# One barrier-free section for the front of the third block, and 64-by-64 inverses of four heads at once

## The reference

```python
h = _layer_norm(x, ln_in_g, ln_in_b)
proj = h @ w_in
pool_in, qkv, z, beta_raw, a_raw, gate_a, gate_b = split(proj)
y_a = _multiscale_pool(pool_in, pool_w, pool_scale)     # windows 2, 4, 8, 16; 4 groups
...
# _gated_deltanet, 8 heads of 128, chunks of 64 tokens
qkv = silu(causal_depthwise_conv(qkv, conv_w))          # 4 taps, 24 tiles of 128 features
q = l2norm(q) * 128 ** -0.5 ; k = l2norm(k)
beta = sigmoid(beta_raw)
g = -exp(a_log) * softplus(a_raw + dt_bias)
a = strict_lower((k*beta) @ k.T * decay) + eye(64)      # one per head and chunk
sol = triangular_solve(a, [v*beta, k*beta*exp(gc)])
# then a scan over the 8 chunks of 64 tokens
...
mixed = sigmoid(gate_a) * y_a + sigmoid(gate_b) * y_b
h = _layer_norm(ALPHA * h + mixed @ w_out, ln1_g, ln1_b)
mlp = square(relu(h @ w_up)) @ w_down                   # and a gated sum, a last layer norm
```

## Time and profile before

| | |
|---|---|
| median of 3 executions | 3611.22 us (3601.39 to 3617.31) |
| the profiled execution | 3615.51 us, of which the span of its instructions is 3613.7 us |
| PE busy | 3304.1 us, 91% of the span |
| PE weight loads busy | 2606.9 us, 72% |
| DVE busy | 1746.7 us, 48% |
| ACT busy | 1216.6 us, 34% |
| POOL busy | 145.5 us, 4% |
| mean granted TensorE clock | 0.937 of full speed |

### The profile page before, as it was taken

How to read it: one execution, slowest core, us unless ns; L and a number is a source line. 1 busy time by engine, 2 the same in 40 slices (tenths; PEclk the granted TensorE clock), 3 DMA queues, 4 the chain that set the end, 5 groups by cost and what they waited for, 6 DMA issues and landing times. The chain is left out here.

```text
span 3613.7 us, 43046 instructions
## 1 busy us (share of the span) xinstructions
PE 3304.1 (91%) x17800; PEld 2606.9 (72%) x17800; DVE 1746.7 (48%) x2642; ACT 1216.6 (34%) x1751; POOL 145.5 (4%) x176
## 2 busy tenths in 40 slices
PE   8999997888699998998999999986977789999998
PEld 6888776667478886876557788865855668778885
DVE  4447536543354456767865333243643334553434
ACT  3333342222533333333443323232345222342323
POOL 0000000120000000000000000000002431000000
PEclk9999997869899999999999999998987988899999
DMA  3336321000223363322012233322220000223332
GB/s 135 97 96 216 111 79 35 2 2 8 82 71 99 117 204 128 97 79 64 1 49 86 82 95 98 99 64 64 88 88 18 19 25 20 75 82 99 94 99 94
DMA packets 76371, 285.23 MB, mean 79 GB/s; under 512 B 8464, under 2 KB 8592, under 8 KB 75152
## 3 DMA queue, kind: packets, MB, share of 16 engines
q1 hardware_dynamic: 76176, 282.47, 24.1%
HBM read 276.15 MB, written 6.29 MB: 78 GB/s over the span
## 5 line engine op out<-in xcount | busy, mean ns | idle before, releaser
L149 DVE TENSOR_TENSOR wlo<-raw,whi 128x1024 fp32r<-128x1024 f32 x450 | 552.2, 1227 | 1238.3 <-ACT whi L144 1238.0
L144 ACT ACTIVATE whi<-raw 128x1024 fp32r<-128x1024 f32 x450 | 475.9, 1058 | 1174.8 <-PE ps L173 1110.6
L171 PE MATMUL ps<-h_hi,wlo 128*128 128x512 f32 x1536 | 621.0, 404 | 51.2 <-PEq L80 21.2
L172 PE MATMUL ps<-h_lo,whi 128*128 128x512 f32 x1536 | 603.5, 393 | 0.0
L173 PE MATMUL ps<-h_hi,whi 128*128 128x512 f32 x1536 | 603.2, 393 | 0.0
L171 PEld LDWEIGHTS ps<-h_hi,wlo 128*128 128x128 f32 x1536 | 291.7, 190 | 130.6 <-issue 54.1
L172 PEld LDWEIGHTS ps<-h_lo,whi 128*128 128x128 f32 x1536 | 292.1, 190 | 62.0 <-issue 5.2
L173 PEld LDWEIGHTS ps<-h_hi,whi 128*128 128x128 f32 x1536 | 291.6, 190 | 62.0
L171 PE MATMUL ps<-mid_hi,wlo 128*128 128x512 f32 x784 | 307.4, 392 | 0.0
L173 PE MATMUL ps<-mid_hi,whi 128*128 128x512 f32 x784 | 305.0, 389 | 0.0
L172 PE MATMUL ps<-mid_lo,whi 128*128 128x512 f32 x784 | 305.0, 389 | 0.0
(11 more groups left out here) (580 smaller groups left out, 5135.9 us busy)
## 6 DMA issues: line engine op xcount, KB each, us to landing
raw<-in_wstream SPq DMA_DIRECT2D x453, 512.0 KB, 3.5
mod_ring<-in_wmod SPq DMA_DIRECT2D x48, 512.0 KB, 4.5
c_rows<-in_c_rows SPq DMA_DIRECT2D x3, 1024.0 KB, 5.6
x<-in_x_t SPq DMA_DIRECT2D x4, 512.0 KB, 7.7
x_saved<-x SPq DMA_DIRECT2D x1, 2048.0 KB, 8.9
x<-x_saved SPq DMA_DIRECT2D x1, 2048.0 KB, 9.1
mix_saved_d<-x SPq DMA_DIRECT2D x1, 2048.0 KB, 8.4
out<-x SPq DMA_DIRECT2D x8, 256.0 KB, 2.1
```

The lines of the kernel that those rows point to most:

```text
L144: act.activation(k.whi[:, n % SPLIT, :], k.raw[:, n % RAW, :], ACT.Copy).then_inc(k.hi_ready, 1)
L149: dve.tensor_tensor(k.wlo[:, n % SPLIT, :], k.raw[:, n % RAW, :], k.whi[:, n % SPLIT, :].bitcast(F32), ALU.subtract).then_inc(k.split_read ...
L171: pe.matmul(out, wlo, hi, start=first, stop=False)
L172: pe.matmul(out, whi, lo, start=False, stop=False)
```

## The change

The parts 1 to 3 above become one section, `branches_front`, with no barrier in it. The stream of weights is reordered for it: `ba`, eight tiles of q, the pool chunk, sixteen tiles of k and v, and then the eight chunks of `gate_a`. The running sums and the squares for the norms move to POOL; norms and pool go beside the q, k and v chunks, transposes and rows beside the `gate_a` chunks. `Background` has no slices there any more; `delta_matrices` takes 4 in each gap instead of 2. `invert` is called twice, for four heads, with 2 slices in each of its ten gaps; the scan keeps its 40.

```diff
-def invert(k, at, xt, tmp, bg=Idle(), slices=(0, 0)):
+def invert(k, at, xt, tmp, bg=Idle(), slices=(0, 0), pairs=4):
...
-        blocks = [(slice(64 * b, 64 * b + 64), slice(64 * p, 64 * p + 64)) for p in range(4) for b in range(2)]
+        tx, out = [k.ps[:, g, 0:width] for g in range(2)], [k.ps[:, 2 + g, 0:width] for g in range(2)]
...
+def branches_front(k, h, qkv, pool_in, mix, k_tok, v_tok, beta, nbeta, g, egc, ekg, egl, mix_d, mix_saved):
...
+        @m.block.gpsimd
+        def _(gp):
...
+            for i, w in enumerate(POOLS):
+                src, width = pool_in[:, i, :], 1
+                if i:
+                    gp.wait_ge(diff, 2 * i)
+                while width < w:
+                    dst = s[:, width.bit_length() % 2, :]
+                    if n:
+                        gp.wait_ge(step, n)
+                    gp.tensor_tensor(dst[:, pad:], src[:, pad:], src[:, pad - width:pad + SEQ - width], ALU.add)\
+                      .then_inc(step, 1)
+                    n += 1
+                    src, width = dst, 2 * width
+            for n in range(2 * DT):
+                gp.wait_ge(silu_done, n + 1)
+                if n >= 2:
+                    gp.wait_ge(sum_ready, n - 1)
+                gp.tensor_tensor(sq[:, n % 2, :], qkv[:, n, :], qkv[:, n, :], ALU.mult).then_inc(sq_ready, 1)
...
+        @m.block.tensor
+        def _(pe):
...
+            def square_sum(n):
+                pe.wait_ge(sq_ready, n + 1)
...
+                if n >= 4:
+                    pe.wait_ge(log_ready, n - 3)
+                    pe.wait_ge(pool_left, DT)
+                pe.matmul(k.ps[:, 4 + n % 4, :], mat(k, "ones"), sq[:, n % 2, :], start=True, stop=True)\
+                  .then_inc(sum_ready, 1)
...
+            def turn(n):
+                src, dst, i, T = tokens[n]
+                pe.wait_ge(normed, 2 * DT)
+                pe.wait_ge(silu_done, 3 * DT)
+                if n >= 2:
+                    pe.wait_ge(copied, n - 1)
+                for c in range(4):
+                    mm = pe.transpose(k.ps[:, 4 + n % 2, c * P:(c + 1) * P], src[:, 4 * i + c, T * P:(T + 1) * P],
+                                      mat(k, "ident"))
+                mm.then_inc(turned, 1)
+            pe.wait_ge(k.split_ready, b0 + 1)
+            chunk(b0, 4)
+            for f in range(3 * DT):
+                if f == DT:
+                    pe.wait_ge(k.split_ready, pool_chunk + 1)
+                    pe.wait_ge(d_lo, 4)
+                    pe.wait_ge(log_ready, 4)
+                    for o in range(DT):
+                        if o >= 4:
+                            pe.wait_ge(pool_left, o - 3)
+                        mm = products(k, pe, pool_chunk, k.ps[:, 4 + o % 4, :], dh[:, o // 2, :], dl[:, o // 2, :],
+                                      o * P, True, True)
+                        mm.then_inc(pool_done if o < DT - 1 else k.chunk_done, 1)
+                pe.wait_ge(k.split_ready, q_chunk(f) + 1)
+                if f >= 4:
+                    pe.wait_ge(pre_ready, f - 3)
+                chunk(q_chunk(f), f % 4)
+                group = (f - 5) // 4
+                if f >= 5 and f % 4 in (1, 2) and group < 4:
+                    first = 4 * group + 2 * (f % 4 - 1)
+                    square_sum(first)
+                    square_sum(first + 1)
+            for i in range(DT):
+                pe.wait_ge(k.split_ready, g0 + i + 1)
...
+                chunk(g0 + i, i % 4)
+                turn(2 * i)
+                turn(2 * i + 1)
+                if i == 3:
...
+                    for T in range(TT):
...
+                if i == 5:
...
+                            pe.matmul(k.ps[:, 7, 32 * b + 8 * T:32 * b + 8 * T + 8], mat(k, name), g[:, T, :],
+                                      start=True, stop=True)
...
+        @m.block.scalar
...
+            next_hi(k, act, b0)
+            act.activation(ba[:, :], k.ps[:, 4, :], ACT.Copy).then_inc(ba_kept, 1)
+            for f in range(3 * DT):
+                if f == DT:
+                    for o in range(DT):
+                        if o < DT - 1:
+                            act.wait_ge(pool_done, o + 1)
+                        else:
+                            next_hi(k, act, pool_chunk)
+                        act.activation(mix[:, o, :], k.ps[:, 4 + o % 4, :], ACT.Copy, scale=col(k, "pool_scale", o))\
+                           .then_inc(pool_left, 1)
+                next_hi(k, act, q_chunk(f))
+                if f == 0:
+                    act.wait_ge(zeroed, 1)
+                act.activation(pre[:, f % 4, 3:], k.ps[:, f % 4, :], ACT.Copy).then_inc(pre_ready, 1)
+                if f in (4, 5):
+                    for i in range(2 * (f - 4), 2 * (f - 3)):
...
+                act.wait_ge(tap_done, 4 * f + 4)
+                act.activation(qkv[:, f, :], qkv[:, f, :], ACT.Silu).then_inc(silu_done, 1)
+                if f >= 6 and f % 4 == 2 and f < 22:
+                    first = f - 6
+                    for n in range(first, first + 4):
+                        act.wait_ge(sum_ready, n + 1)
...
+                        act.activation(rs[:, n % 4, :], k.ps[:, 4 + n % 4, :], ACT.Ln, bias=k.eps[1e-6])\
+                           .then_inc(log_ready, 1)
+                    for n in range(first, first + 4):
+                        act.wait_ge(log_ready, n + 1)
+                        act.activation(rs[:, n % 4, :], rs[:, n % 4, :], ACT.Exp, scale=-0.5).then_inc(rs_ready, 1)
+            act.wait_ge(normed, 2 * DT)
+            for i in range(DT):
+                next_hi(k, act, g0 + i)
+                if i >= 4:
+                    act.wait_ge(mixed, i - 3)
+                act.activation(sig[:, i % 4, :], k.ps[:, i % 4, :], ACT.Sigmoid).then_inc(sig_ready, 1)
+                if i == 0:
+                    act.activation(ba[0:8, :], ba[0:8, :], ACT.Sigmoid).then_inc(beta_ready, 1)
+                if i == 1:
+                    act.activation(na[r, 0:1], col(k, "a_log")[r, :], ACT.Exp).then_inc(a_ready, 1)
...
+                    act.activation(ln[r, :], rc[r, :], ACT.Ln).then_inc(ln_ready, 1)
+                for n in (2 * i, 2 * i + 1):
...
+                    act.wait_ge(turned, n + 1)
+                    act.activation(dst[:, T, 512 * part:512 * part + 512], k.ps[:, 4 + n % 2, :], ACT.Copy)\
+                       .then_inc(copied, 1)
+            act.wait_ge(summed, 1)
...
+        @m.block.vector
         def _(dve):
...
+            def window(i):
+                w, u = POOLS[i], pool_in[:, i, :]
+                src = s[:, (w // 2).bit_length() % 2, :]
+                dve.wait_ge(step, steps[i])
+                dve.scalar_tensor_tensor(d[:, i, 16:], src[:, pad + 16:], 1.0 / w, u[:, pad + 16:], ALU.mult,
+                                         ALU.subtract).then_inc(diff, 1)
...
+            next_lo(k, dve, b0)
+            for f in range(3 * DT):
+                if f == DT:
+                    next_lo(k, dve, pool_chunk)
+                next_lo(k, dve, q_chunk(f))
+                dve.wait_ge(pre_ready, f + 1)
+                o = qkv[:, f, :]
...
+                        dve.tensor_scalar(o, x, w, None, ALU.mult).then_inc(tap_done, 1)
...
+                        dve.scalar_tensor_tensor(o, x, w, o, ALU.mult, ALU.add).then_inc(tap_done, 1)
+                if f < 4:
+                    window(f)
+                if f in (5, 6):
+                    for i in range(2 * (f - 5), 2 * (f - 4)):
+                        dve.wait_ge(d_hi, i + 1)
...
+                if f >= 8 and f % 4 in (0, 1):
+                    first = f - 8 + f % 4
+                    for n in range(first, first + 2):
+                        dve.wait_ge(rs_ready, n + 1)
+                        dve.scalar_tensor_tensor(qkv[:, n, :], qkv[:, n, :], P ** -0.5 if n < DT else 1.0,
+                                                 rs[:, n % 4, :], ALU.mult, ALU.mult).then_inc(normed, 1)
...
+            for i in range(DT):
+                next_lo(k, dve, g0 + i)
+                dve.wait_ge(sig_ready, i + 1)
+                dve.wait_ge(pool_left, i + 1)
+                dve.tensor_tensor(mix[:, i, :], mix[:, i, :], sig[:, i % 4, :], ALU.mult).then_inc(mixed, 1)
+                if i == 1:
...
+            dve.wait_ge(kept, 4)
+            dve.wait_ge(copied, 8)
...
-        with nc.sbuf_tensor(k.name("ba"), [P, 1, SEQ], F32) as ba:
-            dense(k, 1, DT, h, copy_out(k, ba), nothing)
-            bg = Background(k, ctx, 16, h, (6, 7), act_evac, dve_evac)
-            with stage(nc, "sent") as (block, sent):
-                @block.sync
-                def _(sp):
-                    sp.dma_start(mix_d, gate[:, :, :]).then_inc(mix_saved, 16)
-            gate_rows(k, ba, beta, nbeta, g, egc, ekg, egl, bg, 8)
-        norm_tiles(k, [qkv[:, t, :] for t in range(16)], lambda n: (P ** -0.5 if n < 8 else 1.0), 1.0, 1e-6,
-                   bg=bg, slices=4)
```

(56 more changed lines are left out.)

279 lines of the change are left out of this document (124 added, 155 removed).

## The result

The changed kernel takes **3548.7 us** (median of 4 executions, 3542.4 to 3551.5), against 3613.4 for the kernel before beside it. The ratio is 0.9825, interval 0.9808 to 0.9841. Forecast were 3560 and a range of 3530 to 3592. The profiled execution took 3550.1, its span 3548.2, its mean clock 0.942 against 0.937.

What follows compares the result with a forecast made beforehand. PE was taken to idle or run slow in the 531.8 us before the scan, q, k, v paced by an ACT-DVE ring; front 54 us less, matrices and inverses 2 more, so 52 less: 3560, range 3530 to 3592.

Steps and rivals of the forecast that it cites:

- pool chunk: Front, before tile 8's split: PE waits for ACT to empty a bank, then products and a q chunk; 11 us.
- front after Silu 23: Front's end: seven chunks, turns, transposes, row sums, PE restart and a wait, 55.5 us; then the tail, 10.6 us.
- The ring: Front's q, k, v chunks: ACT and DVE taking turns, not PE, set 5.64 us a round; 24 rounds, 135.4 us.
- The port: Front: POOL's 26 sums and squares hold up DVE by 0.4 us each, 10 us in all.
- The head start: Front before the ring starts: `ba` and first q chunk, 2 x 5.44 plus 2.4 for PE's restart, 13.3 us.
- The chunk ends: `delta_matrices`: six chunk ends, four ahead of an exponential at 2.9 us, two in last gaps at 3; 17.6 us.
- The inverses: Inverses: ten levels of 9.4 us for 20 of 4.91, other 10.1 us of each `invert` paid twice; 24 us less.
- the port's full price: Rival, front: each of POOL's 26 instructions costs DVE its full time, 27 us instead of 10; 3577; chance 0.15.
- the dear loads: Rival: each of eight exposed table switches costs its 1.28 us again, 10 us more; 3570; chance 0.02.
- a ring of sums and squares: Rival, front: each norms group waits a round for POOL, PE and ACT in turn; gain about 15 us, 3596; chance 0.05.
- PE at half clock: Rival, front: short idling keeps PE at half clock, 185 us more if in all 34 chunks, 3745; chance 0.03.
- the one where everything hides: Rival: no port cost in the front and chunk ends in the matrices free; 3532; chance 0.15.

Runs made afterwards that it cites:

- e2: Changed kernel with ACT's order turned: it splits tile f before the Silu of tile f-1, norms' groups moved by one tile; 3528.9 us, ratio 0.9777 to the kernel before.
- f3: Changed kernel with one table set holding both Ln and Exp loaded ahead of each group's four Ln; 3545.8 us, ratio 0.9816 to the kernel before.
- f2: Changed kernel with the pool chunk moved in two halves to before tiles 20 and 21, weight stream reordered to match; 3535.7 us, ratio 0.9789.
- e1: Changed kernel with the 16 squares of q and k moved from POOL to ACT's wait for the taps; 3548.9 us, ratio 0.9834 to the kernel before.
- f1: Changed kernel with ACT and DVE emptying a chunk's bank in the matrices after the step's exponentials and products, not before; 3538.4 us, ratio 0.9790.
- f8: f5 with f7's shift of slices added, so no chunk ends in a stage's last gap; 3489.5 us, ratio 0.9650 to the kernel before.
- u1: Changed kernel with the wide inverse undone: four narrow `invert` calls, front and matrices still changed; 3555.5 us, ratio 0.9851 to the kernel before.
- f6: e1 with the ten running sums left out too, so POOL does nothing beside the taps (pool branch computes something else); 3542.5 us, ratio 0.9805.
- f7: Changed kernel with one slice less in the last gap of the second and fourth `delta_matrices`, one more in the scan's second gaps; 3536.7 us, ratio 0.9782.
- f4: Changed kernel with the orders of e2, f1, f2 and f3 together; 3509.1 us, ratio 0.9713 to the kernel before.
- f5: f4 with the pool chunk's halves one tile later, at tiles 21 and 22; 3499.1 us, ratio 0.9683 to the kernel before.

## Why the prediction was right

3560 was 11 us high. Against the profiled execution the sum was 3563.5, measured 3550.1. By stretches all the differences went one way, 3.1 in the front, 2.1 in the matrices, 6.3 in the inverses and 2.0 in the stretches that the change doesn't touch, so the number is not owed to errors that cancel. By its terms:

| term | forecast | measured |
|---|---|---|
| `ba` and first q chunk | 13.3 | 11.0 |
| groups of Ln and Exp, four | 28.6 | 28.9 |
| pool chunk | 11 | 11.1 |
| PE late at tile 10 | 1.3 | 1.4 |
| POOL against DVE | 10 | 10.6 |
| front after Silu 23 | 66.1 | 64.2 |
| the whole front | 265.7 | 262.6 |
| four `delta_matrices` | 96.1 | 94.0 |
| inverses, change | -24 | -30.3 |
| all, change | -52 | -65.5 |

- **The ring.** 5.63 to 5.64 a round where nothing disturbs it (tiles 15 to 18 and 19 to 23). That it is a ring and not PE is shown by e2.
- **What is paid on it.** Norms and pool chunk came to a tenth. f3 shows a load as a part of it, at about its row; f2 shows that half of the pool chunk's 11 were waits for banks, and that the other half moves with the chunk. The measured sum of a row is the excess over 5.64 of the distances that it touches.
- **The port.** 10.6 for 26 instructions, 0.41 each, as I took it. That the sum came out is partly luck, as my even spread was wrong: 8.4 of it fall on the first six rounds. With the squares gone (e1) the ten running sums, one behind the other where DVE has windows to make, cost 5.2 (6.63, 7.28 and 8.22 over 5.63); the squares that queue behind them in the changed kernel most of the rest, and those of the last three groups 2.3. e1 gave 1.7 of its gain back at tiles 6 and 8 (6.68, 17.76). The Trainium skill (SBUF — State Buffer, "SBUF: two separate sides") has the port as an exclusive lock; the trace is in line with that, with the taps of a round at 5.8 in place of 2.8 us beside POOL's rows, and 5.63 or 5.64 in the first five rounds once POOL is idle.
- **Table loads.** f3 rules out the rival by which a switch costs more than its row. The Trainium skill (ScalarE: Activation LUTs, "What ACT_TABLE_LOAD costs") adds a drain of about 1380 ns; a load less gave 1.44 us, its row of 1.28 and little else.
- **The head start** was 2.3 shorter: the `ba` chunk was done 5.6 us after the start, without the 2.4 of a restart that the earlier trace rows had shown. PE had stood 3.2 us ahead of it, and 10.7 in the earlier trace rows. In the changed kernel PE came back at half clock (a matmul every 0.43 us instead of 0.23) after stands of 9.2 and 5.0 us at the pool chunk. No run varied the stand by itself.
- **The chunk ends** were taken at 17.6 for six. The four ahead of an exponential were put at 2.9 each, 11.6; f1 gained 10.9 by taking them out of the way, so the sum was right, but its spread of 0.6, 6.1, 3.5 and 0.6 was not what I had, and that it comes out is luck. f8, which has no end in a last gap and the others behind the exponentials, has its four matrices at 78.3 us, and the forecast without the term was 70.1 + 8.4 = 78.5. By that the ends cost about 15.7, an estimate, since f8 has 46 slices there and not 48 and its clock is another.
- **The inverses** are the step that was mis-sized. A level took 9.11, not 9.4 (ten of them: 2.9 less). The other 3.4 (0.4 of it my rounding of 24.4 to 24) are in the ends, which I copied at 10.1 an `invert`: about 4 of these are a chunk end in the last gap, which before stood in every `invert` and now stands in one of two. I had counted in which stage a chunk ends, not in which gap of it. The four of u1 show the price: 30.7, 29.7 and 30.4 without an end in the last gap, 34.3 with one.

Of the rivals, none came: the port's full price, the dear loads, a ring of sums and squares, PE at half clock (0.91 in the front), and the one where everything hides, 3532, though the result lies nearer to it by what the inverses gave.

## What to carry to other kernels

When PE is fed by a ring of other engines, look for an order in which one engine works an item behind the others, before shortening what is in the ring: here one turned order gave 20 us, and no instruction was taken out. Background work in slices is hidden only if something is left to run when its last slice ends; count in which gap, and at which slice of it, each chunk ends, and put the eviction behind what the foreground waits for. Undo each half of a change by itself: the gain booked to the wide inverse was in good part the place of the chunk ends, and the two halves together gave less than their sum.

## What was unexpected in the hardware

The same 32 small matmuls (the row sums, 16 of 128x8 and 16 of 64x8) were followed by a half-slow chunk in some kernels and by a full-speed one in others. In the changed kernel and in f6, the chunk behind them:

```profile
2683.40:2691.30 7.90, 7.90 (x24) 6.20 (x25) 0.00 (x0) 0.00 (x0) 0.00 (x0) 0.67 0.04 13
```

```profile
2677.00:2682.30 5.30, 5.30 (x24) 4.34 (x24) 0.00 (x0) 0.00 (x0) 0.00 (x0) 1.00 0.19 70
```

At 0.67 PE ran most of it at 1.2 GHz, at 1.00 all of it at 2.4. Split to split across the sums was 12.8 to 12.9 us in the changed kernel, e1, f1, f2, f7 and u1, 11.3 in e2 and f4, and 9.7 in f3, f5, f6 and f8, with the same instructions ahead of it. It belongs to the kernel and is no chance of one execution, as far as four traces tell: the changed kernel, f1, f7 and u1 have the same front, and it took 262.6 in each. What tips it stays open; it moves a kernel by 3 us, as much as some of the edits here.
